# Ring of eight half blocks, cells before rows, and later picks in a hybrid decoder step's expert retrieval

## What is computed

```python
q = (xb @ w_q).reshape(PEER_BLOCK, PEER_HEADS, 2, D_KEY // 2)
s = jnp.einsum('thpc,pnc->thpn', q, sub_keys).astype(jnp.float32)
sv, si = lax.top_k(s, PEER_TOPK)
cand = (sv[:, :, 0, :, None] + sv[:, :, 1, None, :]).reshape(...)
best, flat = lax.top_k(cand, PEER_TOPK)
...
idx = i1 * N_KEYS + i2
gate = jax.nn.softmax(best, axis=-1)
act = jax.nn.gelu(jnp.einsum('thkd,td->thk', u_tab[idx], xb), approximate=False)
coef = (gate * act).astype(xb.dtype)
return jnp.einsum('thk,thkd->td', coef, v_tab[idx])
```

## Time and profile before

| what | us |
|---|---|
| median of 3 runs | 1560.5 (1558.67 to 1567.8) |
| the profiled execution | 1566.55 |
| its span, first to last instruction | 1564.7 |
| mean granted TensorE clock in it | 0.936 of full |
| TensorE busy | 1372.6 (88% of the span) |
| VectorE busy | 1000.1 (64%) |
| ScalarE busy | 667.7 (43%) |
| GpSimd busy | 359.3 (23%) |

### The profile page before, as it was taken

How to read it: one execution, slowest core, us unless ns; L and a number is a source line. 1 busy time by engine, 2 the same in 40 slices (tenths; PEclk the granted TensorE clock), 3 DMA queues, 4 the chain that set the end, 5 groups by cost and what they waited for, 6 DMA issues and landing times.

```text
span 1564.7 us, 24623 instructions
## 1 busy us (share of the span) xinstructions
PE 1372.6 (88%) x8950; PEld 1177.7 (75%) x8950; DVE 1000.1 (64%) x1850; ACT 667.7 (43%) x1492; POOL 359.3 (23%) x284
## 2 busy tenths in 40 slices
PE   6999865998796998899999999999999159799997
PEld 5987632787434988889999999999877147677775
DVE  4556788444523248999327777777677147677776
ACT  4432042231002454344456666666555125455554
POOL 1110131001100015475661000000334743222210
PEclk9999676999888999999999999999999679999998
DMA  6430200000132334444546444444577158888864
GB/s 219 136 120 28 115 16 1 1 1 28 31 161 91 121 100 130 133 139 145 167 140 195 125 126 127 129 126 125 163 257 255 41 195 263 276 272 278 277 217 135
DMA packets 117612, 219.26 MB, mean 140 GB/s; under 512 B 31649, under 2 KB 32161, under 8 KB 116513
## 3 DMA queue, kind: packets, MB, share of 16 engines
q1 hardware_dynamic: 106272, 184.78, 37.5%
q0 software_dynamic: 11264, 33.60, 6.5%
HBM read 207.64 MB, written 10.42 MB: 139 GB/s over the span
## 4 chain that ended last, share of the span: by engine, by line
PE 41%; DVE 10%; POOL 7%; DMA 4%; issue 4%; ACT 3%; SPq 0%; ACTq 0%; DVEq 0%; POOLq 0%
PE ph L1702 9%; PE ph L1703 8%; PE ph L1704 8%; PE acc L1772 4%; POOL RT L1590 4%; PE pg L1753 4%; PE acc L1774 4%; PE acc L1773 4%; DVE ohx L1934 3%; POOL lo L1579 2%; ACT hi L1612 2%; DMA raw<-in_v 2%; DVE lo L1787 1%; DVE hid L1812 1%; DVE hid L1809 1%
## 5 line engine op out<-in xcount | busy, mean ns | idle before, releaser
L1612 ACT ACTIVATE hi<-raw 128x512 fp32r<-128x512 f32 x544 | 341.6, 632 | 483.0 <-PE acc L1774 203.2
L1787 DVE TENSOR_TENSOR lo<-raw,hi 128x512 fp32r<-128x512 f32 x448 | 313.7, 709 | 209.8 <-ACT hi L1612 208.2
L1702 PE MATMUL ph<-xh,hi 128*128 128x320 f32 x1152 | 366.4, 318 | 27.4 <-DVE lo L1787 20.8
L1703 PE MATMUL ph<-xl,hi 128*128 128x320 f32 x1152 | 358.1, 311 | 0.0
L1704 PE MATMUL ph<-xh,lo 128*128 128x320 f32 x1152 | 357.9, 311 | 0.0
L1772 PE MATMUL acc<-hi,ch 128*128 128x512 f32 x512 | 207.6, 405 | 74.8 <-DVE cl L1945 74.7
L1702 PEld LDWEIGHTS ph<-xh,hi 128*128 128x128 f32 x1152 | 218.5, 190 | 33.7 <-DVE lo L1787 22.9
L1703 PEld LDWEIGHTS ph<-xl,hi 128*128 128x128 f32 x1152 | 218.6, 190 | 0.0
L1704 PEld LDWEIGHTS ph<-xh,lo 128*128 128x128 f32 x1152 | 218.1, 189 | 0.0
L1774 PE MATMUL acc<-lo,ch 128*128 128x512 f32 x512 | 201.9, 394 | 0.0
L1773 PE MATMUL acc<-hi,cl 128*128 128x512 f32 x512 | 201.7, 394 | 0.0
(11 more groups left out here) (360 smaller groups left out, 1890.9 us busy)
## 6 DMA issues: line engine op xcount, KB each, us to landing
raw<-in_uT SPq DMA_DIRECT2D x256, 256.0 KB, 2.7
raw<-in_v SPq DMA_DIRECT2D x256, 256.0 KB, 3.1
wraw<-in_w_in SPq DMA_DIRECT2D x30, 512.0 KB, 3.5
raw<-in_w_q SPq DMA_DIRECT2D x32, 256.0 KB, 2.8
wo<-in_w_out SPq DMA_DIRECT2D x4, 1024.0 KB, 10.7
h_scratch<-act_s SPq DMA_DIRECT2D x128, 32.0 KB, 2.5
sth<-in_state_h SPq DMA_DIRECT2D x1, 2048.0 KB, 7.6
out_hgrn_s<-stn SPq DMA_DIRECT2D x1, 2048.0 KB, 6.9
```

Of the source, the lines that this page charges most:

```text
L1612: act.activation(wide(hi[n % 4]), wide(raw[n % 4]), ACT.Copy).then_inc(t_hi, 1)
L1702: pe.matmul(o, hi[s][:, k], xh[:, c], start=begin, stop=False)
L1703: pe.matmul(o, hi[s][:, k], xl[:, c], start=False, stop=False)
L1787: dve.tensor_tensor(wide(lo[n % 4]), wide(raw[n % 4]), wide(hi[n % 4]), ALU.subtract).then_inc(lo_v, 1)
```

## The change

- `hi` and `lo` become rings of eight units (RING); `raw` stays at four. ScalarE runs six units ahead of TensorE's block in Q, A and B, and four to five in V. TensorE's loops are unrolled to eight units.
- In ScalarE's loop over b, `hidden(b - 1)` moves from the end of an iteration to its start, ahead of the scaled one-hots.
- The store to `h_scratch` moves from SP's queue to ScalarE's (`spill`).
- The four row buffers lie in `hid`, over the first 16 coefficient blocks, so GpSimd waits until these are consumed (`c_lo`). All 64 cells are fetched first, then all 64 rows.
- The picks start at v = 38 instead of 10 and come every 4/3 blocks: 38, 39, 40, 42, 43, 44, 46, ... to 122.
- The buffers of the last norm move up by 4 D, and the last sums come some blocks later.

```diff
-        EXP_AT, PICKED = NA // 2 - 4, NA // 2 - 3
-        ACC_AT = {10 + 5 * k // 3: k for k in range(NPICK)}
+        RAW, RING = 4, 8
+        EXP_AT, PICKED = NA // 2 - 4, NA // 4 - 2
+        ACC_AT = {38 + 4 * k // 3: k for k in range(NPICK)}
...
-        hi = [big_mem.sb(f"hi{u}", [P, 4, P], F32R) for u in range(4)]
-        lo = [big_mem.sb(f"lo{u}", [P, 4, P], F32R) for u in range(4)]
+        hi = [big_mem.sb(f"hi{u}", [P, 4, P], F32R) for u in range(RING)]
+        lo = [big_mem.sb(f"lo{u}", [P, 4, P], F32R) for u in range(RING)]
...
-        vbuf = [big_mem.sb(f"vbuf{r}", [P, D]) for r in range(4)]
+        vbuf = [hflat[:, D * r:D * r + D] for r in range(4)]
...
@@ sync: the store leaves this queue
-                    b = (n - UA - 9) // 2
-                    if n % 2 and 0 <= b < NBLK:
-                        sp.wait_ge(hs_done, b + 1)
-                        sp.dma_start(hs_dram[b], act_s[b % 4][:]).then_inc(hs_out[b % 4], 16)
...
@@ gpsimd
                 pool.wait_ge(id_ready, 1)
-                pool.wait_ge(rt_ready, 2)
-                for k in range(4):
-                    rows(k)
                 for r in range(4):
                     pool.wait_ge(hs_out[r], 16 * (NBLK // 4))
-                cells(0, 0, EARLY)
-                for k in range(4, EARLY):
-                    rows(k)
-                cells(1, EARLY, NPICK)
-                for k in range(EARLY, NPICK):
+                for k in range(NPICK):
+                    pool.indirect_dma_start(out=hsel[:, k:k + 1], out_offset=None, in_=hs_cells,
+                                            in_offset=bass.IndirectOffsetOnAxis(ap=cell_id[:, k:k + 1], axis=0)) \
+                        .then_inc(hsel_in, 16)
+                pool.wait_ge(c_lo, 4 * D // DT)
+                for k in range(NPICK):
                     rows(k)
...
@@ scalar
-                    if n >= 4:
-                        act.wait_ge(t_mm, n - 3)
+                    if n >= RING:
+                        act.wait_ge(t_mm, n - RING + 1)
...
+                def spill(b):
+                    act.wait_ge(hs_done, b + 1)
+                    act.dma_start(hs_dram[b], act_s[b % 4][:]).then_inc(hs_out[b % 4], 16)
+
                 for b in range(NBLK):
+                    if b:
+                        hidden(b - 1)
+                    if b == 2 * EXP_AT - 4:
+                        act.wait_ge(e_in, 3)
+                        act.activation(best_flat, best_flat, ACT.Exp).then_inc(e_out, 1)
                     if b >= NA:
                         g = b - NA
                         act.wait_ge(oh_raw, g + 1)
...
                         ins.then_inc(oh_ready, 1)
-                    high(UA + 2 * b + 2)
-                    high(UA + 2 * b + 3)
-                    if b == 2 * EXP_AT:
-                        act.wait_ge(e_in, 3)
-                        act.activation(best_flat, best_flat, ACT.Exp).then_inc(e_out, 1)
+                    high(UA + 2 * b + 6)
+                    high(UA + 2 * b + 7)
+                    if b:
+                        spill(b - 1)
...
-                    if b:
-                        hidden(b - 1)
@@ scalar, stage V
                     act.activation(ch[v % 2][:], hid[:, v], ACT.Copy).then_inc(c_hi, 1)
-                    if v < NBLK - 1:
-                        high(UV + 2 * v + 2)
-                        if v == 0:
-                            hidden(NBLK - 1)
-                        high(UV + 2 * v + 3)
+                    if v == 1:
+                        hidden(NBLK - 1)
+                        spill(NBLK - 1)
+                    if 1 <= v < NBLK - 2:
+                        high(UV + 2 * v + 4)
+                        high(UV + 2 * v + 5)
...
@@ vector, stage V
-                    if v < NBLK - 1:
-                        low(UV + 2 * v + 2)
-                        if v == 0:
-                            times_hidden(NG - 1, NG)
-                        low(UV + 2 * v + 3)
+                    if v == 1:
+                        times_hidden(NG - 1, NG)
+                    if v < NBLK - 2:
+                        low(UV + 2 * v + 4)
+                        low(UV + 2 * v + 5)
```

More of the change, by code:

```diff
@@ L1503, in build_program @@
         v_in = [sem(f"v_in{r}") for r in range(4)]
-        hsel_in = [sem(f"hsel_in{r}") for r in range(2)]
+        hsel_in = sem("hsel_in")
         (keys_in, t_hi, lo_v, lo_p, t_mm, q_ready, s_full, s_ready, e_in, e_out, pk_ready, pt_full, rt_ready, ones_set,
@@ L1573, in _ @@
                 for n in range(UA, UB):
-                    if n == UA + 4 * (PICKED + 1):
+                    if n == UA + 8 * PICKED + 4:
                         pool.wait_ge(rt_ready, 2)
@@ L1583, in rows @@
                         pool.wait_ge(v_used, k - 3)
[L1584 removed]
+                    pool.indirect_dma_start(out=vbuf[k % 4], out_offset=None, in_=v_rows,
                                             in_offset=bass.IndirectOffsetOnAxis(ap=row_id[:, k:k + 1], axis=0)) \
                         .then_inc(v_in[k % 4], 16)
[L1588 to L1592, removed]
                 pool.wait_ge(id_ready, 1)
[L1594 to L1596 removed]
                 for r in range(4):
                     pool.wait_ge(hs_out[r], 16 * (NBLK // 4))
[L1599 to L1603 removed]
+                for k in range(NPICK):
[4 more added lines that the diff above has]
+                for k in range(NPICK):
                     rows(k)
@@ L1619, in scores @@
                     act.activation(scs[half, 2 * (h % 4) + a], pss[half, m % 2, 2], ACT.Copy).then_inc(s_ready, 1)
+                for n in range(6):
+                    high(n)
                 for m in range(NQ + 1):
                     if m < NQ:
-                        high(2 * m)
-                        high(2 * m + 1)
+                        high(2 * m + 6)
+                        high(2 * m + 7)
                     if m >= 1:
@@ L1727, in step_a @@
                 def step_a(i, first):
[L1728 to L1732, removed]
-                        else:
-                            pe.wait_ge(lo_v, i + (WQ + 1))
-                        unit(ph[:, u // 2, 0:NT], u, u % 2)
+                    for u in range(RING):
+                        if u % 2 == 0 and (u >= 4 or not first):
+                            pe.wait_ge(hs_done, 4 * i + (u // 2 - 1))
+                        if u % 4 < 3:
+                            pe.wait_ge(lo_p, 6 * i + (3 * (u // 4) + u % 4 + 1))
+                        else:
+                            pe.wait_ge(lo_v, 2 * i + (WQ + u // 4 + 1))
+                        unit(ph[:, u // 2 % 2, 0:NT], u, u % 2)
                 step_a(0, True)
@@ L1771, in step_v @@
                                 o, cols = acc[:, 2 * t + h], slice(P * t, P * t + P)
-                                pe.matmul(o, ch[c][:, cols], whi, start=first and c == 0, stop=False)
-                                pe.matmul(o, cl[c][:, cols], whi, start=False, stop=False)
-                                ins = pe.matmul(o, ch[c][:, cols], wlo, start=False, stop=last and c == 1)
+                                pe.matmul(o, ch[c % 2][:, cols], whi, start=first and c == 0, stop=False)
+                                pe.matmul(o, cl[c % 2][:, cols], whi, start=False, stop=False)
+                                ins = pe.matmul(o, ch[c % 2][:, cols], wlo, start=False, stop=last and c == 3)
                             ins.then_inc(t_mm, 1)
                 step_v(0, True, False)
-                with pe.Fori(1, NBLK // 2 - 1) as i:
+                with pe.Fori(1, NBLK // 4 - 1) as i:
                     step_v(i, False, False)
-                step_v(NBLK // 2 - 1, False, True)
+                step_v(NBLK // 4 - 1, False, True)
             @block.vector
@@ L1875, in _ @@
                     normalise(best[:, i], PH, picked[:, i, 2]).then_inc(pk_ready, 1)
-                while shared[0] <= PICKED:
+                while shared[0] < 2 * PICKED + 1:
                     share()
```

80 lines of the change are left out of this document (38 added, 42 removed).

## The result

The changed kernel takes 1636.35 us (median of 4 runs, 1630.08 to 1648.94), the kernel before 1559.59 beside it: a ratio of 1.050 (95% interval 1.041 to 1.060). The forecast was 1607.5 with 1578 to 1650 around it: slower, as said, by 77 us where 47 were forecast. The profiled execution took 1631.41 us with a span of 1629.4.

A forecast was written before the change was run, and what follows sets the result against it. TensorE, busy 88% of the span, was taken as the bound. Stage B +128, A -8 and V -73 sum to +47 us, which from the runs' median of 1560.5 gives 1607.5 us, range 1578 to 1650 (8 in 10).

The forecast's parts named there:

- Stage B, +128 us: Stage B: TensorE's next block waits for gelus and scalings behind hidden(b - 1), 2.0 us in each of 64 blocks.
- The cells, -48 us: Stage V: with 64 cells issued first and picks from block 38, the stall on cells goes, -48 us.
- Stage A, -8 us: Stage A: eight units make high early, VectorE's 6.8 us of waits go, less one new lag; -8 us.
- 2.35 us more, once: Stage A: a late share also delays hidden behind high, costing TensorE about 4.1 us instead of 1.75, once.
- The picks, 2.80 us a block: Stage V: fuller DMA makes 85 blocks with picks take 2.80 us, +7 us; four raw slots bind at a 3.8 us landing.
- rival 1: Stage V: DMA-bound picks, loads landing past 3.8 us, 85 blocks at 3.05 us or worse; +28 instead of +7, chance 0.12.
- The late `cl`, -29 us: Stage V: with high a block earlier, cl is no longer late behind picks, 0.28 us a block over 105 blocks.
- Block 64, -3 us: Stage V: the 1.8 MB loaded at block 64 meet fuller DMA but a deeper ring; 8 us lost instead of 11.
- Late in V, 0: End of stage V: the last sums and late losses, 9 us before, stay at 9; change 0.
- Rival 2: Stage B: TensorE's clock falls because it idles 1.8 us in every 6.4; 64 us more, 1671, chance 0.08.
- Rival 3: Not slower: the ring takes away every TensorE wait outside B, A -37 and V -97; 1554, chance 0.05.
- Rival 4: Stage V: cells come later than the first pick, cl waits behind it, 15 us; 1622, chance 0.07.

The follow-up runs named there:

- run 1: The changed kernel with ScalarE scaling the one-hots before hidden(b - 1) in stage B again; 1505.96 us, 0.962 of the kernel before.
- run 2: The kernel before, ring of four, with only hidden(b - 1) moved to the start of ScalarE's iteration; 1690.59 us in one run.
- run 3: The kernel before with all cells fetched first, picks at 38 + 4k/3 and the last sums late as in the changed kernel; 1512.9 us, one run.
- run 7: The kernel of run 1 with ScalarE four units ahead instead of six in stages Q, A and B; 1500.76 us, ratio 0.966.
- runs 5 to 7: Run 1 with residual rows and norm weights loaded before block 38 (1494.63 us); that with rows spread among cells, picks from block 19 (1497.77 us); run 7.
- run 11: The kernel of run 7 with residual rows and norm weights loaded early and four more raw slots from block 44 of V; 1461.57 us, ratio 0.940.
- run 10: The kernel of run 3 with eight raw slots, row buffers in hid, and residual loads at blocks 25 to 31; 1492.7 us, ratio 0.958.
- run 4: The changed kernel with only 4 of 64 row fetches, all 64 picks still done; 1610.1 us in one run, V 356.8 us.

## Why the prediction was right, and where its size was off

- **Stage B, +128 us: right, to a microsecond.** 2.0 us in each of 64 blocks by place, chain and size; +128.3 in the profile, undone by run 1 and made again by run 2. The rows gave 1.95 and the forecast was rounded to 2.0; that it hit 2.0 so closely is luck within the 1.8 to 2.2 that it allowed.
- **The cells, -48 us: right as far as shown.** No wait of 40 us; run 3 gives 46 for cells and picks together, with the denser picks already in it. The two were not taken apart.
- **Stage A, -8 us: it did not come.** The profiled pair has +3 in Q + A, which is no more than the spread. The split of share 18 (719.65 us, shown above) tells the two halves of the term apart. It starts 225.3 us after Q opens, before it was 228.4: 3.1 us of VectorE's 6.8 came. The waits for `hi` at shares 2 and 13 did not go away but grew shorter (2.31 and 1.19 us). The ring lets `high` run ahead only as far as the four raw slots do: ScalarE waited for u's loads 104 us (59 times) in stage A, before it was 46 (29 times). From share 18 to the end of A the forecast had 97.3 us (2.35 + 92.5 + 2.5); it took 105.6, before 99.2. The step that failed is "2.35 us more, once". TensorE waited for `act_s` 11 times, 9.9 us, and 8 us of that lie ahead of share 18, where the prediction charged nothing. So TensorE comes to share 18 with more left: 665 matmuls to the end of A instead of 652. Behind it are 1.9 us of waits for `act_s`, 1.8 for GpSimd's split, 1.7 for the first scalings of B, and a granted clock of 0.98 in the mean instead of 1.00. With a lead of four it is 653 matmuls and 101.4 us, as run 7 shows; how the rest divides is open.
- **The picks, 2.80 us a block: too low, it is 2.94 to 3.08.** The threshold was right: "At 3.8 it binds". Loads landed in 3.8 us after the change (median, 1440 to 1590 us) and 4.0 to 4.3 in runs 5 to 7, where the sum used 3.2. 0.14 us over 85 blocks is 12 us. That makes it rival 1 in its place (loads late in four slots), at less than its price of 28. Its reading that slots and not bytes limit holds: run 11 moves the bytes faster. Its pointer to the ceiling of the Trainium skill's page does not (last point below).
- **The late `cl`, -29 us: right in size, but hidden.** The ring of eight removes it and meets the slots, so it shows 11 to 13 us. With eight slots the ring is worth 379.3 - 351.5 = 28 us (run 10 against run 11, which also differ in the layout of the slots).
- **Block 64, -3 us: wrong sign.** 16 us lost instead of 11, and 8 without the rows. That the 1.8 MB met four slots already late is argued from this.
- **Late in V, 0: too careful.** 9 us of losses were left in the sum. The last 30 us did 129 matmuls, 29 us of work: almost nothing was lost.
- V in all: -59.5 against -73: 12 more for the picks, 8 more at block 64, some 8 fewer at the end. The sum is +65 in the profiles against +47. Everything but B was forecast at -81; run 1, which has B as it was, measures -57 against the kernel before beside it (1505.96 - 1562.83), so "near 1480" was 26 too low. B hit its mark; the other terms together are 24 us off, which is most of the 29 us between 1607.5 and the result.
- Rival 2 (the clock) is out: TensorE idled 1.74 us in every 6.42 and kept 1.00. Its price was also low: in the earlier trace rows the rate falls with the grant (17 matmuls in 3.64 us at 0.67, 4.7 per us against 6.88), so 4.41 us of work wholly at half the clock would be an estimated 4.4 us more, not 3. Rival 3 is out in this kernel: A gave nothing. Rival 4 is out: VectorE did not wait for cells.
- The 358 GB/s of the Trainium skill ("DMA: Bandwidth & Descriptors", Specifications) would have held V near 13 us above; run 11 is 3 us above and moved 370 GB/s over 20 us. The measurement decides against it here. The prediction took the figure without its condition: the same page says, under "Measured (HBM→SBUF, 128 partitions, SWDGE, issued from GpSimd)", that about 358 is each core's share when both cores of a pair stream. This kernel runs on one core.

## What to carry to other kernels

Where an engine works in order, look at what each moved instruction now stands in front of: a step that waits for the end of TensorE's block must not come before one that TensorE needs to start the next. A deeper ring pays in full only when the ring that feeds it is deep enough too (11 us here against 28). Hold the slots against the landing time under the new load, not that of the kernel before. And when two limits lie at nearly the same pace, removing either shows only a part (10 or 11 us of some 40 here), so test the pair before giving up.

## What the runs showed that was not expected

- The start of the retrieval moves by 13 us between executions (488.5 to 501.9) with the same instructions ahead of it.
- The DMA engines held 340 GB/s for 200 us and 370 for 20 at a busy share of 0.98 to 1.00 (run 11), with a landing of 5.9 to 6.3 us for 256 KB, which took 2.7 us at 194 GB/s (run 4). A share of 0.85 to 0.88 with about 300 GB/s looked like a ceiling in six kernels and was none.
- Gaps of 1.74 us in each 6.42 us, for 400 us on end, left TensorE's granted clock at 1.00, its level of 2.4 GHz (stage B after the change).
